# First front panels and first queries multiplied ahead of the norm's root, in a hybrid encoder trunk

## The reference

```python
def rmsnorm(x, g, eps=1e-6):
    xf = x.astype(jnp.float32)
    y = xf * lax.rsqrt(jnp.mean(xf * xf, axis=-1, keepdims=True) + eps)
    return (y * g.astype(jnp.float32)).astype(x.dtype)

def peer_ffn(hn, wq, sub_keys, u, v):
    ...
    q = (hn @ wq).reshape(bsz, seq, PEER_HEADS, 2, PEER_KEY_DIM)
    sc = jnp.einsum("bshpc,hpnc->bshpn", q, sub_keys).astype(jnp.float32)
    v1, i1 = lax.top_k(sc[..., 0, :], PEER_TOPK)
    ...

for l in range(DEPTH):
    h = h + hybrid_mixer(rmsnorm(h, norm_mix_g[l]), w_in[l], ...)
    h = h + memory_cross_attention(rmsnorm(h, norm_xa_g[l]), mem, ...)
    h = h + peer_ffn(rmsnorm(h, norm_ffn_g[l]), peer_wq[l], peer_keys[l], ...)
```

## Time and profile before

| | us |
|---|---|
| median of 3 runs | 4185.61 (4175.88 to 4195.9) |
| the profiled execution | 4188.13 |
| its span, first to last instruction | 4186.3 |
| TensorE busy | 3982.1 (95%) |
| VectorE busy | 2810.4 (67%) |
| ScalarE busy | 1699.2 (41%) |
| GpSimd busy | 1349.1 (32%) |

### The profile page before, as it was taken

The page is one execution under the profiler, slowest core; times in us unless marked ns, Lnnn a source line. Parts: engine busy times, 40 slices in busy tenths (PEclk is TensorE's granted clock), DMA queues, the critical chain, the costliest instruction groups (busy, mean ns, idle before and its releaser), DMA issues.

```text
span 4186.3 us, 59338 instructions
## 1 busy us (share of the span) xinstructions
PE 3982.1 (95%) x19746; PEld 3411.6 (81%) x19746; DVE 2810.4 (67%) x4322; ACT 1699.2 (41%) x3110; POOL 1349.1 (32%) x890
## 2 busy tenths in 40 slices
PE   7998999989999999999999899999899999999998
PEld 5666878779999988888866678777799999888886
DVE  1684331499988977787716833316999889777776
ACT  2522123224666653433325231332256666534333
POOL 5343553411212432222243345624112124322231
PEclk9998999989999999999999999999899999999999
DMA  3111322226878999999721123312278789999995
GB/s 125 46 61 64 107 91 86 86 73 226 298 268 310 360 373 344 347 350 342 280 69 50 56 83 103 106 61 91 91 249 295 264 295 393 372 354 359 337 348 190
DMA packets 360973, 879.42 MB, mean 210 GB/s; under 512 B 27857, under 2 KB 191953, under 8 KB 353873
## 3 DMA queue, kind: packets, MB, share of 16 engines
q1 hardware_dynamic: 153360, 508.20, 33.9%
q0 software_dynamic: 73728, 268.47, 17.0%
q10 hardware_dynamic: 133696, 100.67, 8.0%
HBM read 774.47 MB, written 102.76 MB: 210 GB/s over the span
## 4 chain that ended last, share of the span: by engine, by line
PE 69%; DVE 15%; issue 4%; DVEq 4%; DMA 3%; ACT 2%; ACTq 2%; POOL 0%; SPq 0%
PE ps L1152 41%; PE ps L1435 19%; PE ps L1412 3%; DVE conv L815 2%; DVE wlo L759 2%; DMA raw<-in_experts 1%; PE ps L1160 1%; ACTq L483 1%; DVE ubuf L1014 1%; DVE acc L1021 1%; DMA act_e<-early_gelu 1%; DVEq L935 1%; DVEq L777 1%; PE ps L1200 1%; PE ps L1286 1%
## 5 line engine op out<-in xcount | busy, mean ns | idle before, releaser
L1152 PE MATMUL ps<-xhi,whi 128*128 128x384 f32 (+1 forms) x3328 | 1229.3, 369 | 111.0 <-DVE xlo L773 30.8
L1152 PE MATMUL ps<-xlo,whi 128*128 128x384 f32 (+1 forms) x3328 | 1197.5, 360 | 0.0
L1152 PE MATMUL ps<-xhi,wlo 128*128 128x384 f32 (+1 forms) x3328 | 1197.3, 360 | 0.0
L1152 PEld LDWEIGHTS ps<-xhi,whi 128*128 128x128 f32 x3328 | 635.3, 191 | 188.9 <-issue 66.1
L456 ACT ACTIVATE whi<-raw 128x1024 fp32r<-128x1024 f32 x618 | 647.3, 1054 | 319.9 <-PE ps L1435 223.2
L759 DVE TENSOR_TENSOR wlo<-raw,whi 128x1024 fp32r<-128x1024 f32 x512 | 622.0, 1218 | 170.7 <-ACT whi L456 166.8
L1152 PEld LDWEIGHTS ps<-xlo,whi 128*128 128x128 f32 x3328 | 636.2, 191 | 52.6 <-issue 4.8
L1152 PEld LDWEIGHTS ps<-xhi,wlo 128*128 128x128 f32 x3328 | 634.7, 191 | 53.4
L416 POOL DMA_INDIRECT ubuf<-in_up_rows,gidx x256 | 290.9, 1137 | 1103.8 <-DVE small L1014 908.3
L1435 PE MATMUL ps<-whi,eh 128*128 128x512 f32 x1536 | 601.6, 392 | 27.3 <-DVE el L1113 27.2
L1435 PE MATMUL ps<-wlo,eh 128*128 128x512 f32 x1536 | 599.3, 390 | 0.0
(11 more groups left out here) (200 smaller groups left out, 4785.5 us busy)
## 6 DMA issues: line engine op xcount, KB each, us to landing
raw<-in_experts SPq DMA_DIRECT2D x512, 512.0 KB, 6.4
raw<-in_back SPq DMA_DIRECT2D x112, 512.0 KB, 3.2
gate_table<-gbuf SPq DMA_DIRECT2D x48, 1024.0 KB, 9.1
act_e<-early_gelu ACTq DMA_DIRECT2D x128, 384.0 KB, 7.1
gtile<-gate_table ACTq DMA_DIRECT2D x30, 1536.0 KB, 23.5
raw<-in_front SPq DMA_DIRECT2D x64, 512.0 KB, 3.2
raw<-in_gates SPq DMA_DIRECT2D x48, 512.0 KB, 3.2
early_gelu<-weighted SPq DMA_DIRECT2D x128, 192.0 KB, 5.7
```

The costliest lines, as they stand in the source:

```text
L1152: ins = MM(out, w[:, a:a + P], x[:, c, t0:], start=(i == 0 and n == 0), stop=(i == len(chunks) - 1 and n == 2))
```

## The change

At two places of each layer, the front and the queries, TensorE multiplies first on `uhi` and `ulo`, the halves of `h` times the gain, without the root. ScalarE makes `uhi` and VectorE `ulo`, chunk by chunk. `early_linears` goes chunk after chunk through all panels at once (four front panels in banks 0 to 3, or three queries in banks 0 to 2), and the sums of the squares are put between the chunks. The results are multiplied by the reciprocal of the root as VectorE takes them out of PSUM (`qT`, with the factor 0.125, and the first three `pqT`). Meanwhile the normalised `xhi` and `xlo` are made as before, for all later panels. In the front the banks go on as 4, 5, 6, 0, 1 and so on (`front_bank`). At the queries the sums of chunks 0 to 5 move between the last output panels, `residual` and the low half of each chunk alternate on VectorE, and the order becomes query 3, score 0, score 1, query 4, score 2, query 5, score 3, score 4, and then as before.

```diff
+        uhi = (place("uhi0", E, [KC, T], F32R), place("uhi3", F, [KC, T], F32R))
+        ulo = (place("ulo0", E + KC * T * 4, [KC, T], F32R), place("ulo3", F + KC * T * 4, [KC, T], F32R))
...
+        def front_bank(n):
+            return n if n < 7 else n - 7
...
+            def early_norm(L, k, g, done, count):
+                u = k // 3
+                for c in range(KC):
+                    act.wait_ge(done, count + c + 1)
+                    A(uhi[u][:, c, :], h[:, c, :], ACT.Copy, scale=pc(g, c)).then_inc(uhi_ready, 1)
+                    n = k * KC + c
+                    act.wait_ge(sq_used, L * NORMS + (n - 1 if n >= 2 else 0))
+                    A(sq[:, c % 2, :], h[:, c, :], ACT.Square).then_inc(sq_ready, 1)
+                act.wait_ge(sq_used, L * NORMS + (k + 1) * KC)
+                A(std[:, :], ps[:, 7, :], ACT.Sqrt, scale=1.0 / D, bias=eps6).then_inc(std_ready, 1)
+                for c in range(KC):
+                    act.wait_ge(xf_ready, L * NORMS + k * KC + c + 1)
+                    A(xhi[:, c, :], xf[:, c % 2, :], ACT.Copy).then_inc(xhi_ready, 1)
...
-                norm(L, 0, lambda c: h[:, c, :], T, xhi, L * KC)
-                for i in range(12):
+                early_norm(L, 0, "mix_g", h_final, L * KC)
+                act.wait_ge(qkv_copied, L * 12 + 4)
+                for i in range(4, 12):
...
-                act.wait_ge(h_ready, (L + 1) * ROUNDS)
-                norm(L, 3, lambda c: h[:, c, :], T, xhi)
...
+                early_norm(L, 3, "ffn_g", h_ready, L * ROUNDS + KC)
+                for l in range(3):
+                    panel(l, L, base + 8)
+                    round_panel(l, L, base + 9)
+                panel(3, L, base + 8)
+                act.wait_ge(pq_copied, L * LISTS + 3)
+                act.wait_ge(score_done, L * LISTS + 2)
+                A(pqT[:, 1, :], ps[:, 3, :], ACT.Copy).then_inc(pq_copied, 1)
...
+            def early_lo(L, u, g, c):
+                dve.wait_ge(uhi_ready, L * (2 * KC) + u * KC + c + 1)
+                STT(out=ulo[u][:, c, :], in0=h[:, c, :], scalar=pc(g, c), in1=uhi[u][:, c, :].bitcast(F32),
+                    op0=ALU.mult, op1=ALU.subtract).then_inc(ulo_ready, 1)
...
+                for c in range(KC):
+                    early_lo(L, 0, "mix_g", c)
...
+                for i in range(4):
+                    panel(i, L, 0)
+                    STT(out=qT[:, i, :], in0=ps[:, i, :], scalar=0.125, in1=std[:, :], op0=ALU.mult, op1=ALU.mult).then_inc(qkv_copied, 1)
...
-                residual(FRONT // 4 + KC + 8)
+                for c in range(KC):
+                    residual(FRONT // 4 + KC + 8, range(c, c + 1))
+                    drain()
+                    early_lo(L, 1, "ffn_g", c)
                 norm(L, 3, lambda c: h[:, c, :], T, "ffn_g", xlo, xhi)
+                for l in range(3):
+                    panel(l, L, G1 + 10)
+                    if l == 2:
+                        dve.wait_ge(score_done, L * LISTS + 1)
+                    TT(pqT[:, l % 2, :], ps[:, l, :], std[:, :], ALU.mult).then_inc(pq_copied, 1)
...
+            def early_linears(L, u, n, use, free, stats):
+                for c in range(KC):
+                    pe.wait_ge(ulo_ready, L * (2 * KC) + u * KC + c + 1)
+                    for s in range(n):
+                        if c == 0:
+                            pe.wait_ge(split[s], L * USES + use + 1)
+                            if free is not None:
+                                pe.wait_ge(h_ready, free + s + 1)
+                        a = SLOT[s] + c * P
+                        for q, (w, x) in enumerate(((whi, uhi[u]), (whi, ulo[u]), (wlo, uhi[u]))):
+                            ins = MM(ps[:, s, :], w[:, a:a + P], x[:, c, :], start=(c == 0 and q == 0), stop=(c == KC - 1 and q == 2), skip_group_check=True)
+                        if c == KC - 1:
+                            ins.then_inc(used[s], 1)
+                    norm(L, 3 * u, T, stats[c])
...
-                norm(L, 0, T)
-                for s in range(4):
-                    linear(s, L, 0, ps[:, s, :], xhi, xlo, each=None if s else (xlo_ready, L * NORMS))
-                with pe.Fori(1, 3) as i:
-                    for s in range(4):
-                        pe.wait_ge(qkv_copied, L * 12 + i * 4 - (3 - s))
-                        linear(s, L, i, ps[:, s, :], xhi, xlo)
+                early_linears(L, 0, 4, 0, None, [range(2 * c, 2 * c + 2) if c < 4 else range(0) for c in range(KC)])
+                for n in range(4, 12):
+                    if n >= 7:
+                        pe.wait_ge(qkv_copied, L * 12 + n - 6)
+                    linear(n % 4, L, n // 4, ps[:, front_bank(n), :], xhi, xlo, each=(xlo_ready, L * NORMS) if n == 4 else None)
...
-                norm(L, 3, T)
+                    norm(L, 3, T, (range(0, 4), range(0), range(4, 5), range(5, 6))[s])
+                early_linears(L, 1, 3, G1 + 10, L * ROUNDS + KC + 4, [range(6 + c, 7 + c) if c < 2 else range(0) for c in range(KC)])
                 pe.wait_ge(h_ready, (L + 1) * ROUNDS)
-                pe.wait_ge(std_ready, L * 4 + 4)
...
-                query(0)
-                for l in range(1, LISTS):
+                query(3)
+                score(0)
+                score(1)
+                query(4)
+                score(2)
+                pe.wait_ge(std_ready, L * 4 + 4)
+                query(5)
+                score(3)
+                score(4)
+                for l in range(6, LISTS):
                     query(l)
                     score(l - 1)
```

More of the change, by code:

```diff
@@ L248, in build_trunk @@
             sem(n) for n in ("sq_ready", "sq_used", "std_ready", "xf_ready", "xhi_ready", "xlo_ready"))
+        uhi_ready, ulo_ready = sem("uhi_ready"), sem("ulo_ready")
         h_ready = sem("h_ready")
@@ L488, in _ @@
                 act.wait_ge(par_loaded, (L + 1) * 16)
-                norm(L, 0, lambda c: h[:, c, :], T, xhi, L * KC)
-                for i in range(12):
+                early_norm(L, 0, "mix_g", h_final, L * KC)
+                act.wait_ge(qkv_copied, L * 12 + 4)
+                for i in range(4, 12):
                     panel(i % 4, L, i // 4)
-                    A((qT, kT, vT)[i // 4][:, i % 4, :], ps[:, i % 4, :], ACT.Copy, scale=0.125 if i < 4 else 1.0).then_inc(qkv_copied, 1)
+                    A((kT, vT)[i // 4 - 1][:, i % 4, :], ps[:, front_bank(i), :], ACT.Copy).then_inc(qkv_copied, 1)
                 for b in range(TB):
@@ L619, in _ @@
                 xo_copies(3)
-                act.wait_ge(h_ready, (L + 1) * ROUNDS)
-                norm(L, 3, lambda c: h[:, c, :], T, xhi)
[L623 to L628, removed]
+                early_norm(L, 3, "ffn_g", h_ready, L * ROUNDS + KC)
[6 more added lines that the diff above has]
+                A(pqT[:, 1, :], ps[:, 3, :], ACT.Copy).then_inc(pq_copied, 1)
+                round_panel(3, L, base + 9)
+                with act.Fori(1, LISTS // 4) as i:
+                    for s in range(4):
+                        panel(s, L, i + (base + 8))
+                        act.wait_ge(score_done, L * LISTS + i * 4 + (s - 1))
+                        A(pqT[:, s % 2, :], ps[:, s, :], ACT.Copy).then_inc(pq_copied, 1)
+                        round_panel(s, L, i + (base + 9))
                 act.wait_ge(xt_turned, L * 2 + 1)
@@ L990, in _ @@
                 for l in range(LISTS):
-                    hold(score_done, L * LISTS + l + 1)
+                    hold(score_done, (L + 1) * LISTS - (LISTS - 1 - l))
                     scores = [ps[:, 4 + l % 4, tb * NK:(tb + 1) * NK] for tb in range(TB)]
@@ L1125, in _ @@
                 for c in range(KC):
-                    dve.wait_ge(acc_turned, L * KC + c + 1)
+                    dve.wait_ge(acc_turned, (L + 1) * KC - (KC - 1 - c))
                     TT(h[:, c, :], h[:, c, :], ps[:, OUT_BANK[c], :], ALU.add).then_inc(h_final, 1)
@@ L1154, in linear, with norm @@
                     ins.then_inc(used[s] if done is None else done, 1)
-            def norm(L, k, w):
-                for c in range(KC):
+            def norm(L, k, w, part=range(KC)):
+                for c in part:
                     pe.wait_ge(sq_ready, L * NORMS + k * KC + c + 1)
                     MM(ps[:, 7, 0:w], cst("ones"), sq[:, c % 2, 0:w], start=(c == 0), stop=(c == KC - 1)).then_inc(sq_used, 1)
+            def early_linears(L, u, n, use, free, stats):
[12 more added lines that the diff above has]
+                    norm(L, 3 * u, T, stats[c])
             pe.wait_ge(consts_ready, 4)
@@ L1359, in query @@
                         pe.wait_ge(pq_copied, L * LISTS + l - 3)
-                    linear(l % 4, L, G1 + 10 + l // 4, ps[:, l % 4, :], xhi, xlo, each=None if l else (xlo_ready, L * NORMS + 3 * KC))
+                    linear(l % 4, L, G1 + 10 + l // 4, ps[:, l % 4, :], xhi, xlo, each=(xlo_ready, L * NORMS + 3 * KC) if l == 3 else None)
                 def score(l):
```

## The result

| | before | after |
|---|---|---|
| median, us | 4181.28 (6 runs) | 4198.09 (6 runs) |
| range of the runs, us | 4175.88 to 4195.9 | 4194.7 to 4200.01 |
| profiled execution, us | 4188.13 | 4197.66 |

The changed kernel takes 1.0034 times as long, with an interval of 1.0019 to 1.0049: 14 us slower by the ratio, 17 us by the medians. The prediction had 15 us less. Its sign is wrong, and the time lies outside its range.

The account below looks back on a forecast made before the run. TensorE, busy 95%, was taken to bound the kernel, VectorE the query stage. Front terms +1.6 (layer 0) and -6.3 (layer 1), queries -5.2 in each layer, sum to -15.1 us: 4171 us, range 4154 to 4186 (8 in 10).

Parts of the forecast that it names:

- Front of layer 1: TensorE starts at about 2096.8 instead of 2109.58, panel 4 at 2129.8 instead of 2136.1: a gain of 6.3 us.
- the fall and rise of the clock in it: New front loop, after idle time: 5 us at half speed, a loss of 2.5 us, bounds 0 and 5.
- the new wait of 1.9 us for the cut: Both fronts: the four slots come free together, so panel 4 waits some 1.9 us for GpSimd's cut.
- The rival by which changing banks every three matmuls keeps the clock down: New loops: TensorE idles between groups at the lower clock; up to 93 us more, 4264 us; chance 0.04.
- waits for `inds`: End of the query stage: TensorE's waits for this VectorE output grow from 11.7 to 17 to 25 us a piece.
- The normalised chunks are in time: Fronts: last `xlo` comes 5.1 us after the end of panel 3, panel 4 wants it 6.7 us after.
- The last rival: Panel 4 and query 3 wait for a late last `xlo`, 3 us each: -3 us, 4182 us; chance 0.08.
- lie beside the output panels: Queries: eight low halves on VectorE, some 0.75 us each, covered by output panels of 5.44 us each.
- the four sums: Queries: sums of chunks 0 to 3 behind the first of the last four output panels cost 4.0 us.
- T + 31.2: Queries: start of MAX8 of list 0, counted from T, the old end of the last output panel; before, T + 32.4.
- The lists: Queries: four VectorE waits of 0.99 us vanish, 5.38 us a list, list 4 at T + 52.7 instead of T + 57.9.
- 1.6 were foretold: Front of layer 0: panel 4 starts at 56.3 instead of 54.7, a loss of 1.6 us.

Follow-up runs that it names:

- q_sums: Kernel before with the changed queries, sums of chunks 2 and 3 moved behind the second of the last four output panels: 4175.65 us, ratio 0.9982.
- act_dve: Kernel after, with panels 4 to 7 rounded by ScalarE and their low halves made by VectorE instead of GpSimd: 4175.39 us, ratio 0.9988 to the kernel before.
- pool_set: Kernel before, with twelve unused GpSimd memsets from the root of each layer's first norm on: 4182.43 us in a single execution, beside 4179.95.
- q_only: Kernel before with the changed queries and its own old front: 4180.4 us, ratio 0.9992 to the kernel before.
- hold_cuts: Kernel after, with GpSimd's cut of panel 4 begun only when the last `xlo` is made: 4197.68 us, ratio 1.0036 to the kernel before.

## Why the prediction was wrong, step by step

**Right.** Front of layer 1: the layer arrives 6.15 us late (2088.78 to 2094.93), and with that the start was foretold at 2102.95; it came at 2102.94. Panel 4's start, 2129.8 + 6.15 = 2135.95, came at 2135.97, so the length of the loop, the fall and rise of the clock in it (0.77 over the first 9 us) and the new wait of 1.9 us for the cut (measured 2.01) are all right together. The rival by which changing banks every three matmuls keeps the clock down did not happen: TensorE is busy for 18.00 of 18 us at a granted clock of 1.00 in the new loop. Queries: VectorE is the limit there as foretold, and lists 1 to 4 no longer wait for TensorE. TensorE's gain went into its waits for `inds`, 19.2 and 17.0 us, 18.1 a layer where 17 to 25 were named; before they were 11.7.

**The step that failed** is the sentence "The normalised chunks are in time". It took `xf` and `xlo` from the earlier trace rows, 9.5 us for eight chunks, and asked when they would be made; it did not ask what would then run beside them. In the same paragraph the cuts of panels 4 to 7 were put at that very time. Before, GpSimd was idle during the chain: the chain ran from 25.90 to 37.50 us in layer 0, and GpSimd stood still from 25.29 us to its cut of panel 4:

```profile
38.65 1.04 POOL L377 CAST whi<-raw 128x1024 fp32r<-128x1024 f32 x1 [13.35 <-PE ps L1152]
```

(The cut at 44.11 us in the earlier trace rows is that of panel 5.) Once the cuts began, each chunk of the pair cost 4.2 us, not 1.44, and panel 5 began 16.6 us after the end of panel 3 in layer 1 (2150.58 from 2133.96), where the prediction had 1.9 + 5.4 = 7.3. That is 9.3 us. The rest of the 12.0 in layer 1 comes behind the start of panel 5: the granted clock from 2150.6 to 2156.0 us is 0.60, so 4.3 of these 5.4 us are at the lower level, which costs 2.2 us. In layer 0 the cuts also slowed the beginning (the fourth panel of the loop starts at 26.13 us instead of 25.3; `ulo` stands beside them), panel 4 starts at 57.95 instead of 56.3, and the mean granted clock beside panel 4 is 0.66: 13.2 us more than foretold.

The last rival had this place, "the last chunk of `xlo` comes late and panel 4 and query 3 wait", with margins of 1.6 and 1.0 us and a chance of 0.08. Its place was right for panel 4, its price of 3 us was too small, for it named no cause of the lateness and so had no duration to multiply. Query 3 did not wait: no cuts stand beside the chain there.

**The sums of the queries.** The same lock acts once more. The prediction said that the eight low halves "lie beside the output panels", at 0.75 us each. VectorE after, layer 1:

```profile
2840.32 0.68 DVE L941 TENSOR_TENSOR h<-h,ps 128x512 f32<-128x512 f32 x1
2841.79 2.56 DVE L817 SCALAR_TENSOR_TENSOR ulo<-h,par,uhi 128x512 fp32r<-128x512 f32 x1 [0.79 <-ACT uhi L485]
2844.26 0.67 DVE L941 TENSOR_TENSOR h<-h,ps 128x512 f32<-128x512 f32 x1
```

A low half takes 2.56 us beside a cut, and the residual of chunk 3 is queued behind it. Its square is late, and TensorE's fourth sum waits the 1.98 us that `q_sums` takes away. So the four sums cost 5.8 us and not 4.0. MAX8 of list 0 came at T + 33.0 instead of T + 31.2. That the long `ulo` delays the residual is borne out by `act_dve`: there the second `ulo` takes 0.75 us, the residual behind it starts at 2809.61 us, 2.2 us behind the one before it where it is 4.1 in the kernel after, and the four sums take the 4.00 us that the prediction had.

**The lists.** The prediction counted a removed wait at its full 0.99 us, 6.37 - 0.99 = 5.38 for a list. VectorE after, list 1 of layer 1:

```profile
2896.34 0.89 DVE L1043 MAX8 vals<-ps 128x8 f32<-128x128 f32 x4 [0.21 <-issue]
...
2901.93 0.50 DVE L1043 MAX8 vals<-ps 128x8 f32<-128x128 f32 x2 [0.21 <-issue]
```

5.59 us a list (the view of the second row ends within it): 0.21 us of each wait stays as the time between instructions, though nothing is waited for. Four lists, 0.84 us. With 1.8 for the sums it is 2.6 of the 3.0 us missing in each layer.

**The reference that the prediction measured from.** The front of layer 1 takes 91.67 us in the trace of before, but 89.60, 89.49 and 89.53 in `pool_set`, `q_only` and `q_sums`, whose front is the same work. The difference lies in the squares and their sums. Windows, first of before, then of `q_only`:

```profile
2091.66:2103.10 11.44, 9.08 (x16) 3.12 (x16) 2.19 (x9) 6.18 (x9) 2.81 (x2) 0.85 0.28 95
2079.80:2089.00 9.20, 7.52 (x16) 2.46 (x16) 2.11 (x9) 6.20 (x9) 2.74 (x2) 1.00 0.34 118
```

So 2.1 us of the 6.3 that the prediction gained in layer 1 belonged to that one execution, in which TensorE's clock was at 0.85 there. Against the other three the changed front costs 7.8 us in layer 1 and not 5.66, and that of `act_dve` gains 3.4 and not 5.5. With its +4.4 in layer 0 the front of `act_dve` comes out at +1.0 in its profiled execution, about even.

**What stays open.** With the lock gone from the front, layer 0 still loses 4.4 us where 1.6 were foretold. Panel 4 starts on time there (56.39 us, foretold 56.3) but takes 8.06 us instead of 5.44, with 1.9 us in four short waits for VectorE: cut and chain stand in one queue. Whether another order would give back these 2.6 us was not tried. Why the clock of the execution of before was lower in that one place is not shown.

## What to carry to other kernels

A duration from a trace holds for the neighbours that it had. When a chain on VectorE is moved, list what GpSimd does at the new time: if it reads SBUF and the VectorE instruction has both inputs there, a price near the sum of the two is right and not that of the longer one (here 1.44 + 3.57 = 5.0 us for a pair and a cut, measured 4.2). Which of the two pays more went by which began first, and in `act_dve` 0.3 us turned it. Whether a kernel may already pay for this is seen in the spread of one instruction's durations: a row with a median of 0.75 and a maximum of 3.8 us for one shape is such a case. The remedy is another engine for one of the two, as in `act_dve`, rather than a wait that only puts them one after the other, as in `hold_cuts`. And take the duration that you move from more than one trace: here 2.1 us of the gain foretold in one layer stood in one execution only.

## What the runs showed of the hardware

- Beside a subtraction of GpSimd that began before it, a 128x512 `TENSOR_TENSOR` with both inputs in SBUF took 2.83 us instead of 0.69 and `SCALAR_TENSOR_TENSOR` 2.67 instead of 0.75; beside its cast `SCALAR_TENSOR_TENSOR` took 1.35. GpSimd pays too: its cast took 1.50 instead of 1.04, and a subtraction that began 0.09 us behind VectorE 2.93 instead of 2.40. Twelve memsets of GpSimd cost VectorE nothing.
- With one of the two inputs in PSUM nothing was longer: all 48 additions to `h` in the kernel after took 0.67 to 0.69 us, 40 of them beside a GpSimd instruction.
- The trace of before held it already, in a row that the prediction does not use: the taps of the convolution on VectorE (ns: least, median, most). All 44 taps of over 0.9 us lie beside a cut of GpSimd, and 174 of the 196 short ones beside nothing of it.

```profile
L815 DVE SCALAR_TENSOR_TENSOR conv<-upad,par,conv x240: 750/752/3821, 138.0 to 2390.9; 128x512 f32<-128x512 f32 x120
```

- The granted clock was 1.00 for 18 us in a loop that changes its PSUM bank every three matmuls, and fell to 0.66 and 0.77 over panel 4, where matmuls came in groups with up to 3.2 us of waiting between.
